# The last four gate quarters moved behind the first pair's scores, and one quarter ahead of every half batch of cached values

## The chip, the cores and the metric

The kernel runs on one core of one Trainium2 chip. The metric is the device time of one execution in microseconds; of before there are three timed runs, and one more execution that the hardware profiler recorded. The engines are named as in the profile: PE (TensorE matmuls), PEld (its weight loads), DVE (VectorE), ACT (ScalarE), POOL (GpSimd) and SP (SyncE, which only issues DMAs here).

## The reference, cut to what matters

One decoder layer for 512 prompt tokens and 8 x 4 sample tokens with the same weights. What the change touches is the part between the input projection and the output merge:

```
z = x @ w_in + b_in                     # q, k, v, conv pair ua/ub, gate_logits (2 x 1024 columns)
q, k = partial_rotary(q), partial_rotary(k)
u = ua * sigmoid(ub); conv = silu(layer_norm(causal_depthwise(u)))
prompt: s = q.k of 3 dilated groups, masked softmax, p @ v, groups merged by softmax denominators
sample: the same over cached keys and values, 8 batches, plus the 4 new tokens
y = (sigmoid(gA) * (attn @ w_attn_out) + sigmoid(gB) * (conv @ w_conv_out)) @ w_o
h = layer_norm(alpha*x + y);  out = layer_norm(alpha*h + moe(h))     # 32 experts, top 2
```

`gate_logits` are not needed before the merge. Their projection is the filler work that this change places differently.

## The kernel before, in words

Every engine has an instruction stream of its own, executed in the order in which it is written, and waits on semaphores. The program has these stages, by the profile's time: the input projection of 26 column tiles (to 171 us), the middle stage in which the gates are projected, q and k are rotated, and both attentions are computed (171 to 412 us), the merge with two projections, the first layer norm and the routing (to some 538 us), the loop over 32 experts, and the last layer norm.

**The middle stage.** The gate projection is cut into 64 quarters (`gate_quarter(q)`, L603): one unit `u = q // 2` is one 128-column tile of the gates over half of the tokens (272 of 544), eight matmuls deep, and a quarter is four of these (the profile shows each of them as two records, so a quarter is `x8`). Unit `u` accumulates in PSUM bank `u % 2`, signals `gate_mm` when its second quarter ends, and ACT copies it out with the bias (`gate_unit`, L1082), which signals `gate_free`. The first quarter of a unit waits until the unit two before it has been copied out.

A list, `order`, written out by hand in L369 to L384, sets what stands between the quarters. Each entry is (step, index, number of quarters ahead of it). PE, ACT and DVE walk the same list, each doing its own part of a step. The steps are:

- `conv_rows`: transposes of the last rows of the convolution's input (L613, L615).
- `rotate` 0 to 11 (L626): one matmul pair with the rotation matrix for each tile of q and k. DVE adds the parts (L1356 to L1359). The step's wait (`rot_used`) keeps PE at most two tiles ahead of DVE, whose first operation of each tile frees the bank pair. DVE comes to `rotate` only when it has finished the depthwise convolution (L1343), a loop that began under the projection.
- `values` 0 to 5 (L637): transposes of v; the first waits until DVE has rotated all 12 tiles (`rotated`).
- `sample_rows`, `cached_keys` 0 to 15 (L675), `keys`, `new_keys`, `sample_turn`, `sample_probs`: the sample attention up to its probabilities.
- `cached_values` 0 to 15 (L738): six matmuls of 8 or 2 columns each for each half batch, in banks 6 and 7; for the first two also three matmuls of 64 columns (L730).
- `conv_mean`, `conv_square`, `conv_var`, `conv_root`, `conv_silu`: the layer norm over channels, between half batches 3 and 13.
- `attend` 0 to 9: the prompt attention of 16 (row block, head) items in pairs. `scores(2p)` (L760, L762) writes banks 0 to 3 for two items; DVE masks and takes the maximum (L1437, L1439), ACT exponentiates (L1151), DVE normalises (L1445, L1446); `turn(i)` (L772) transposes the probabilities into banks 4 and 5, ACT copies them to SBUF (L1144), and `weigh(i)` (L786) multiplies them with the values. `turn(i)` for i of 1 and more waits for ACT's copy of the item before (`pt_act`), since both use banks 4 and 5.

In the list of before, `attend` 0 stands ahead of the last two half batches, and all 64 quarters stand ahead of `attend` 0. The convolution and the rotations get 7 + 12 quarters, `values` 7, the first three half batches of cached values 2 each, the others up to half batch 13 one each, and the last two none.

**Around it.** SP loads the weights of 8 quarters at a time, 8 quarters ahead. It loads `w_conv_out`, `w_o` and the first expert's weights when all 32 units are through (`gate_mm` of 32), because these overwrite the projection's operands. POOL issues the loads of cached keys and values four batches ahead.

Of the kernel before, what the change touches and what calls it, by code (L numbers as in the profile page):

```python
# [21 lines left out]
ACT = mybir.ActivationFunctionType  # L22
AX_X = mybir.AxisListType.X

P = 128
D = 1024
KD = D // P
SEQ, NB, NT = 512, 8, 4
NS = NB * NT
N = SEQ + NS  # L30
HALF = N // 2
# [78 lines left out]
def build(nc, a, o):  # L110
# [14 lines left out]
    with ExitStack() as ctx:  # L125
# [3 lines left out]
        def sem(name):  # L129
            return ctx.enter_context(nc.semaphore(name))  # L130
# [18 lines left out]
        ps = ctx.enter_context(nc.psum_tensor("ps", [P, 8, 512], F32))  # L149
# [11 lines left out]
        wring = eb[:, 0:4096].rearrange("p (s k n) -> p s k n", s=2, k=KD)  # L161
# [17 lines left out]
        zr = z2[:, :].rearrange("p (m n) -> p m n", n=N)  # L179
# [137 lines left out]
        gate_mm, gate_free, gate_sig = sem("gate_mm"), sem("gate_free"), sem("gate_sig")  # L317
# [48 lines left out]
        U_TILES = [2 * pair + c for pair in U_PAIRS for c in range(2)]  # L366


        order = [("conv_rows", 0, 7)] + [("rotate", m, 1) for m in range(12)] + [("values", m, 2 if m == 0 else 1) for m in range(6)]  # L369
        order.append(("sample_rows", 0, 1))  # L370
        for i in range(2 * NB):
            order.append(("cached_keys", i, 1))
# [2 lines left out]
        order += [("new_keys", 0, 0), ("sample_turn", 0, 1), ("sample_probs", 0, 3)]  # L375
        norm = {3: "conv_mean", 5: "conv_square", 7: "conv_var", 9: "conv_root", 12: "conv_silu"}
        for i in range(2 * NB):
            if i == 2 * NB - 2:
                order.append(("attend", 0, 0))
            order.append(("cached_values", i, (2 if i < 3 else 1) if i < 2 * NB - 2 else 0))  # L380
            if i in norm:
                order.append((norm[i], 0, 0))

        order += [("attend", p, 0) for p in range(1, 10)]  # L384
        assert sum(step[2] for step in order) == 4 * 16
        starts = np.cumsum([0] + [step[2] for step in order]).tolist()
        steps = [(kind, i, range(q, q + n)) for (kind, i, n), q in zip(order, starts)]

        STORES = 3 + 1 + NT + 3 * NT


# [151 lines left out]
        def _(pe):  # L543
# [27 lines left out]
            for h in range(2):  # L571
                pe.wait_ge(x_loaded[h], 32)
                for n in range(2):
                    for half in range(2):
                        for k in range(4 * h, 4 * h + 4):
                            last = pe.matmul(ps[:, 2 * n + half, 0:HALF], wring[:, 0, k, n * P:(n + 1) * P], xt[:, k, half * HALF:(half + 1) * HALF],
                                             start=k == 0, stop=k == KD - 1, skip_group_check=True)
# [13 lines left out]
            def gate_quarter(q):  # L591

                u = q // 2
                t, half, j = u // 2, u % 2, 13 + u // 4
                if q % 8 == 0:
                    pe.wait_ge(win_loaded[j % 2], 16 * (j // 2 + j % 2))
                if u < 2 and q % 2 == 0:

                    pe.wait_ge(tile_free, 2 + 25)
                elif q % 2 == 0:  # L600
                    pe.wait_ge(gate_free, u - 1)
                for k in range(4 * (q % 2), 4 * (q % 2) + 4):
                    last = pe.matmul(ps[:, half, 0:HALF], wring[:, j % 2, k, (t % 2) * P:(t % 2 + 1) * P],  # L603
                                     xt[:, k, half * HALF:(half + 1) * HALF], start=k == 0, stop=k == KD - 1, skip_group_check=True)
                if q % 2 == 1:
                    last.then_inc(gate_mm, 1)
# [138 lines left out]
            def scores(i):  # L745

                r, h = divmod(i, HEADS)
                hp = h // 2
                if i == 0:

                    pe.wait_ge(cnorm, 1)
                    pe.wait_ge(gate_free, 32)
                else:
                    pe.wait_ge(pmax, i)
                for g in range(3):
                    for odd in range(2):
                        rows, bank = slice(64 * odd, 64 * odd + 64), 2 - 2 * odd
                        q = zqkv[rows, Q0 + 2 * g + hp, r * P:(r + 1) * P]
                        if g == 0:
                            pe.matmul(ps[:, bank, :], q, zqkv[rows, K0 + hp, 0:SEQ], start=True, stop=True)  # L760
                            continue
                        last = pe.matmul(ps[:, bank + 1, (g - 1) * P:g * P], q, zqkv[rows, K0 + 2 * g + hp, r * P:(r + 1) * P],  # L762
                                         start=True, stop=True)
                        if g == 2:
                            last.then_inc(qk_ps, 1)

            def turn(i):
                pe.wait_ge(pnorm, i + 1)
                if i >= 1:
                    pe.wait_ge(pt_act, i)  # L770
                for c in range(6):
                    last = pe.transpose(ps[:, 4 + c // 3, (c % 3) * P:(c % 3 + 1) * P], prob[:, i % 4, c * P:(c + 1) * P], eye)  # L772
                last.then_inc(pt_ps, 1)
# [40 lines left out]
            for m in range(KD):  # L814
# [3 lines left out]
                for half in range(2):  # L818
# [3 lines left out]
                    for k in range(2):  # L822
                        last = pe.matmul(ps[:, s + 2 + half, 0:HALF], wa[:, k, m * P:(m + 1) * P], at[:, k, cols], start=k == 0, stop=k == 1)
# [84 lines left out]
            for t in range(NTT - 1):  # L908
                last = counts(t)
# [122 lines left out]
        def _(ac):  # L1032
# [29 lines left out]
            for n in range(8):  # L1062
                if n % 2 == 0 and n >= 2:

                    j = n // 2 + 1
# [12 lines left out]
            def gate_unit(u):  # L1078

                t, half = divmod(u, 2)  # L1080
                ac.wait_ge(gate_mm, u + 1)
                ac.activation(zr[:, 8 + t, half * HALF:(half + 1) * HALF], ps[:, half, 0:HALF], ACT.Identity,  # L1082
                              bias=colb[:, G0 + t:G0 + t + 1]).then_inc(gate_free, 1)

            def conv_rows(_):
# [857 lines left out]
```

## Time and profile before

| | us |
|---|---|
| timed runs, median of 3 (lowest to highest) | 1170.38 (1165.73 to 1170.91) |
| the profiled execution | 1171.49 |
| its span, first to last instruction | 1169.2 |
| PE busy in the span | 1107.1 (95%) |
| DVE busy | 841.0 (72%) |
| ACT busy | 581.9 (50%) |
| mean granted TensorE clock | 0.966 of full speed |

[...] A "busy" PE is one with an instruction under way; in the chain of waits each piece of time is given to the instruction or the releaser that the next step had to wait for, so the chain's durations of consecutive PE instructions add up without overlap, while those of a timeline overlap a little.

### The profile page before, as it was taken

To read this page: it belongs to the slowest core of one execution; us is meant where nothing else is said; L and a number is where in the kernel's file an instruction comes from. 1 tells how busy PE (TensorE), PEld (TensorE's weight loads), DVE (VectorE), ACT (ScalarE), POOL (GpSimd) and SP (SyncE) were. 2 spreads that over 40 slices of the span, in tenths; PEclk is the share of its full clock that TensorE was granted. 3 is DMA by queue.
4 is the path that set the end of the run, shared out by engine and by line. 5 is a ranking of instruction groups with operands and counts; after the bars stand their busy time and mean duration, and the time that the engine had idled before them with its cause. 6 is when DMAs were issued, how large, how long until landed. Compare 5 with 4: busy or idle time off the path is not lost.

```text
span 1169.2 us, 16215 instructions
## 1 busy us (share of the span) xinstructions
PE 1107.1 (95%) x6020; PEld 886.8 (76%) x6020; DVE 841.0 (72%) x988; ACT 581.9 (50%) x523; POOL 263.1 (22%) x185
## 2 busy tenths in 40 slices
PE   8999999999999999994999999999999999999970
PEld 7999998889888888863677777777777777777750
DVE  1699999500025728575799998888898888888857
ACT  2322211111115661003677778778777787787740
POOL 2453520000000015001032331332322323323200
PEclk8999999999998999995999999999999999999995
DMA  7468723235424440327799999999999999999824
GB/s 262 151 261 316 273 106 120 99 131 177 136 82 157 167 150 1 113 84 308 266 358 375 366 378 357 355 359 361 352 364 367 359 358 357 362 358 367 315 43 152
DMA packets 40481, 293.06 MB, mean 251 GB/s; under 512 B 10944, under 2 KB 14656, under 8 KB 24830
## 3 DMA queue, kind: packets, MB, share of 16 engines
q1 hardware_dynamic: 26173, 262.53, 59.4%
q0 software_dynamic: 10720, 25.98, 7.6%
q10 hardware_dynamic: 3552, 4.06, 1.1%
q8 instruction: 25, 0.41, 0.1%
q14 instruction: 11, 0.08, 0.0%
HBM read 286.83 MB, written 41.12 MB: 280 GB/s over the span
## 4 chain that ended last, share of the span: by engine, by line
PE 92%; DVE 4%; DMA 2%; issue 1%; ACT 0%; POOLq 0%; SPq 0%; DVEq 0%
PE ps L603 10%; PE ps L950 10%; PE ps L952 10%; PE ps L951 10%; PE ps L974 5%; PE ps L976 5%; PE ps L975 5%; PE ps L558 4%; PE ps L556 4%; PE ps L557 4%; PE ps L821 3%; PE ps L933 2%; PE ps L786 2%; PE ps L675 2%; PE ps L867 2%; PE ps L869 2%
## 5 line engine op out<-in xcount | busy, mean ns | idle before, releaser
L1675 DVE TENSOR_TENSOR region_b_split<-region_b,z_split 128x2048 fp32r<-128x2048 f32 x96 | 216.9, 2287 | 25.7 <-ACT z_split L1203 25.6
L1675 DVE TENSOR_TENSOR region_a_split<-region_a,z_split 128x2048 fp32r<-128x2048 f32 x96 | 216.7, 2286 | 23.2 <-ACT z_split L1203 23.1
L950 PE MATMUL ps<-z_split,scratch_split 128*96 128x512 f32 x512 | 206.2, 403 | 1.9 <-DVE scratch_split L1680 1.9
L952 PE MATMUL ps<-z_split,scratch_split 128*96 128x512 f32 x512 | 201.6, 394 | 0.0
L1203 ACT CAST z_split<-region_a 128x2048 fp32r<-128x2048 f32 x96 | 179.9, 1909 | 0.0
L1203 ACT CAST z_split<-region_b 128x2048 fp32r<-128x2048 f32 x94 | 176.2, 1908 | 2.0 <-PE ps L952 2.0
L1343 DVE SCALAR_TENSOR_TENSOR z_conv_gates<-scratch,column_vectors,z_conv_gates 128x512 f32<-128x512 f32 x240 | 142.8, 674 | 0.0
L603 PE MATMUL ps<-x_columns,region_b 128*128 128x272 f32 x512 | 129.4, 400 | 0.0
L558 PE MATMUL ps<-z_split,region_b_split 128*128 128x272 f32 x384 | 111.2, 290 | 0.0
L556 PE MATMUL ps<-z_split,region_b_split 128*128 128x272 f32 x384 | 110.8, 288 | 0.0
L952 PEld LDWEIGHTS ps<-z_split,scratch_split 128*96 128x96 f32 x512 | 83.0, 162 | 36.4
L950 PEld LDWEIGHTS ps<-z_split,scratch_split 128*96 128x96 f32 x512 | 85.1, 166 | 33.7 <-DVE scratch_split L1680 2.2
L557 PE MATMUL ps<-z_split,region_b_split 128*128 128x272 f32 x384 | 110.4, 287 | 0.0
L603 PEld LDWEIGHTS ps<-x_columns,region_b 128*128 128x128 f32 x512 | 95.5, 193 | 17.8
L974 PE MATMUL ps<-z_split,x_columns_split 128*96 128x512 f32 x256 | 101.0, 395 | 2.0 <-issue 1.2
L951 PE MATMUL ps<-region_b_split,scratch_split 128*96 128x512 f32 x256 | 101.0, 395 | 0.0
L976 PE MATMUL ps<-z_split,x_columns_split 128*96 128x512 f32 x256 | 100.9, 394 | 0.0
L951 PE MATMUL ps<-region_a_split,scratch_split 128*96 128x512 f32 x256 | 100.6, 393 | 0.0
L1778 POOL TENSOR_TENSOR region_b_split<-region_b,region_b_split 128x1024 fp32r<-128x1024 f32 x24 | 64.4, 2705 | 75.8 <-ACT region_b_split L1057 75.7
L1082 ACT ACTIVATE z_conv_gates<-ps,column_vectors 128x272 f32<-128x272 f32 x32 | 15.6, 488 | 123.3 <-PE ps L603 123.1
L1839 POOL DMA_INDIRECT expert_rows<-value_rows,block_rows x26 | 67.6, 2598 | 23.2 <-POOL block_rows L1836 23.2
L557 PEld LDWEIGHTS ps<-z_split,region_b_split 128*128 128x128 f32 x384 | 72.4, 189 | 0.0
(260 smaller groups left out, 1778.7 us busy)
## 6 DMA issues: line engine op xcount, KB each, us to landing
region_b<-in_w_expert_gate SPq DMA_DIRECT2D x16, 2048.0 KB, 12.7
region_a<-in_w_expert_up SPq DMA_DIRECT2D x16, 2048.0 KB, 13.0
region_a<-in_w_expert_gate SPq DMA_DIRECT2D x16, 2048.0 KB, 12.7
region_a<-in_w_expert_down SPq DMA_DIRECT2D x16, 2048.0 KB, 12.6
region_b<-in_w_expert_up SPq DMA_DIRECT2D x16, 2048.0 KB, 13.5
region_b<-in_w_expert_down SPq DMA_DIRECT2D x16, 2048.0 KB, 12.5
region_b<-in_w_in_pairs SPq DMA_DIRECT2D x20, 1024.0 KB, 4.8
region_b<-in_cache_tiles POOLq DMA_DIRECT2D x16, 768.0 KB, 4.9
```

The source lines that it names most:

```text
L556: pe.matmul(out, w_hi[:, s, k, tile], x_hi[:, k, cols], start=k == 0, stop=False)
L557: pe.matmul(out, w_hi[:, s, k, tile], x_lo[:, k, cols], start=False, stop=False)
L558: last = pe.matmul(out, w_lo[:, s, k, tile], x_hi[:, k, cols], start=False, stop=k == KD - 1)
L603: last = pe.matmul(ps[:, half, 0:HALF], wring[:, j % 2, k, (t % 2) * P:(t % 2 + 1) * P], xt[:, k, half * HALF:(half + 1) * HALF], start=k ...
L950: pe.matmul(out, xh[:, k, :], hi[:, k, :], start=k == 0, stop=False)
L951: pe.matmul(out, xh[:, k, :], lo[:, k, :], start=False, stop=False)
L952: last = pe.matmul(out, xl[:, k, :], hi[:, k, :], start=False, stop=k == KD - 1)
L974: pe.matmul(out, hh[:, k, :], hi[:, k, cols], start=k == 0, stop=False)
L976: last = pe.matmul(out, hl[:, k, :], hi[:, k, cols], start=False, stop=k == KF - 1)
L1203: ac.copy(high_part[w][:, part], raw[place][:, part]).then_inc(high_set[w], 1)
L1343: ve.scalar_tensor_tensor(dst, win(k), wdw_c[:, bass.ds(k * CT + c, 1)], dst, ALU.mult, ALU.add).then_inc(conv_step, 1)
L1675: ve.tensor_tensor(low_part[place][:, part], raw[place][:, part], high_part[high or w][:, part].bitcast(F32), ALU.subtract).then_inc(low_s ...
```

## The change

The quarters are spread over the list in another way, and the last four get other PSUM banks.

- `conv_rows` has 5 quarters ahead of it, no longer 7; `values` 0 has 1, no longer 2; the first three half batches of cached values have 1 each, no longer 2.
- The last two half batches have 1 quarter each, no longer none, and stand ahead of `attend` 0.
- `attend` 1 has the last 4 quarters (units 30 and 31) ahead of it; they stand behind `attend` 0's scores. These two units accumulate in banks 4 and 5, the banks of the turns, and wait for no bank. `scores(0)` therefore waits for 30 units copied out instead of 32, and `turn(0)` for all 32.

```diff
-        order = [("conv_rows", 0, 7)] + [("rotate", m, 1) for m in range(12)] + [("values", m, 2 if m == 0 else 1) for m in range(6)]
+        order = [("conv_rows", 0, 5)] + [("rotate", m, 1) for m in range(12)] + [("values", m, 1) for m in range(6)]
...
         for i in range(2 * NB):
-            if i == 2 * NB - 2:
-                order.append(("attend", 0, 0))
-            order.append(("cached_values", i, (2 if i < 3 else 1) if i < 2 * NB - 2 else 0))
+            order.append(("cached_values", i, 1))
...
-        order += [("attend", p, 0) for p in range(1, 10)]
+        order += [("attend", p, 4 if p == 1 else 0) for p in range(10)]
...
+        GATE_BANK = [u % 2 for u in range(30)] + [4, 5]
...
                 u = q // 2
+                bank = GATE_BANK[u]
...
-                elif q % 2 == 0:
+                elif q % 2 == 0 and u < 30:
                     pe.wait_ge(gate_free, u - 1)
...
-                    last = pe.matmul(ps[:, half, 0:HALF], wring[:, j % 2, k, (t % 2) * P:(t % 2 + 1) * P],
+                    last = pe.matmul(ps[:, bank, 0:HALF], wring[:, j % 2, k, (t % 2) * P:(t % 2 + 1) * P],
...
                     pe.wait_ge(cnorm, 1)
-                    pe.wait_ge(gate_free, 32)
+                    pe.wait_ge(gate_free, 30)
...
                 pe.wait_ge(pnorm, i + 1)
-                if i >= 1:
+                if i == 0:
+                    pe.wait_ge(gate_free, 32)
+                else:
                     pe.wait_ge(pt_act, i)
...
-                ac.activation(zr[:, 8 + t, half * HALF:(half + 1) * HALF], ps[:, half, 0:HALF], ACT.Identity,
+                ac.activation(zr[:, 8 + t, half * HALF:(half + 1) * HALF], ps[:, GATE_BANK[u], 0:HALF], ACT.Identity,
```

**PE around the first rotations.** L603 is a gate quarter (4 matmuls here), L613 and L615 are `conv_rows`, L626 is `rotate`. Before:

```order
L603 MATMUL ps<-x_columns,region_b 128x272 [waits gate_free]
L603 MATMUL ps<-x_columns,region_b 128x272 x7
L603 MATMUL ps<-x_columns,region_b 128x272 [waits gate_free]
L603 MATMUL ps<-x_columns,region_b 128x272 x3
L613 MATMUL ps<-const_small,scratch 30x128 [waits state_sb,u_set]
```

```order
L626 MATMUL ps<-region_a,const_small 128x272 x2
L603 MATMUL ps<-x_columns,region_b 128x272 x4
L626 MATMUL ps<-region_a,const_small 128x272 [waits rot_used]
L626 MATMUL ps<-region_a,const_small 128x272
L603 MATMUL ps<-x_columns,region_b 128x272 [waits gate_free]
```

And now, the same place in the program:

```order
L603 MATMUL ps<-x_columns,region_b 128x272 [waits gate_free]
L603 MATMUL ps<-x_columns,region_b 128x272 x3
L613 MATMUL ps<-const_small,scratch 30x128 [waits state_sb,u_set]
L613 MATMUL ps<-const_small,scratch 30x128 x3
L615 MATMUL ps<-const_small,region_a 32x128 x4
L603 MATMUL ps<-x_columns,region_b 128x272 x4
L626 MATMUL ps<-region_a,const_small 128x272 [waits tile_free]
L626 MATMUL ps<-region_a,const_small 128x272
L603 MATMUL ps<-x_columns,region_b 128x272 [waits gate_free]
L603 MATMUL ps<-x_columns,region_b 128x272 x3
L626 MATMUL ps<-region_a,const_small 128x272 x2
```

Behind the run of quarters, `conv_rows` now follows after two quarters fewer. From there on the two orders are alike to the last rotation: one quarter between two of them, and `rot_used` waited for from `rotate` 2 on.

**PE from the last rotation to the first values (L637).** Before:

```order
L626 MATMUL ps<-region_a,const_small 128x272 [waits rot_used]
L626 MATMUL ps<-region_a,const_small 128x272
L603 MATMUL ps<-x_columns,region_b 128x272 x4
L603 MATMUL ps<-x_columns,region_b 128x272 [waits gate_free]
L603 MATMUL ps<-x_columns,region_b 128x272 x3
L637 MATMUL ps<-const_small,region_a 128x128 [waits rotated]
```

Now:

```order
L626 MATMUL ps<-region_a,const_small 128x272 [waits rot_used]
L626 MATMUL ps<-region_a,const_small 128x272
L603 MATMUL ps<-x_columns,region_b 128x272 x4
L637 MATMUL ps<-const_small,region_a 128x128 [waits rotated]
L637 MATMUL ps<-const_small,region_a 128x128 x3
```

One quarter instead of two stands between the last rotation and the step that waits for DVE's last rotation.

**PE at the last half batches and the first pair.** L738 is `cached_values`, L760 and L762 are `scores`, L772 (now L774) is `turn`, L786 (now L788) is `weigh`. Before:

```order
L760 MATMUL ps<-region_a 128x512 [waits gate_free,cnorm]
L760 MATMUL ps<-region_a 128x512
L762 MATMUL ps<-region_a 128x128 x4
L738 MATMUL ps<-w_attn,region_b 128x8 [waits cache_loaded3]
L738 MATMUL ps<-w_attn,region_b 128x2 x4
L738 MATMUL ps<-w_attn,region_b 128x8 x2
L738 MATMUL ps<-w_attn,region_b 128x2 x4
L738 MATMUL ps<-w_attn,region_b 128x8
L760 MATMUL ps<-region_a 128x512 [waits pmax]
L760 MATMUL ps<-region_a 128x512
L762 MATMUL ps<-region_a 128x128 x4
L772 MATMUL ps<-const_small,scratch 128x128 [waits pnorm]
```

Now:

```order
L603 MATMUL ps<-x_columns,region_b 128x272 x4
L738 MATMUL ps<-w_attn,region_b 128x8
L738 MATMUL ps<-w_attn,region_b 128x2 x4
L738 MATMUL ps<-w_attn,region_b 128x8
L760 MATMUL ps<-region_a 128x512 [waits gate_free,cnorm]
L760 MATMUL ps<-region_a 128x512
L762 MATMUL ps<-region_a 128x128 x4
L603 MATMUL ps<-x_columns,region_b 128x272 x16
L760 MATMUL ps<-region_a 128x512 [waits pmax]
L760 MATMUL ps<-region_a 128x512
L762 MATMUL ps<-region_a 128x128 x4
L774 MATMUL ps<-const_small,scratch 128x128 [waits gate_free,pnorm]
```

The 12 short matmuls between the first two pairs' scores are gone from there, and 16 gate matmuls stand in their place.

## Rows read from the trace of the kernel before

**Rows 1.** Page, part 4: the chain that ended last, by engine

```profile
PE 92%; DVE 4%; DMA 2%; issue 1%; ACT 0%; POOLq 0%; SPq 0%; DVEq 0%
```

**Rows 2.** Windows of PE: start:end us, length, busy (x), clock, DMA share, GB/s

```profile
238.70:289.80 51.10, 51.10 (x337) 1.00 0.54 173
311.40:314.84 3.44, 3.44 (x9) 0.50 0.45 135
316.90:360.40 43.50, 43.50 (x267) 1.00 0.17 56
366.05:372.85 6.80, 5.82 (x30) 0.50 0.65 238
374.00:412.00 38.00, 38.00 (x334) 1.00 0.48 195
410.00:430.00 20.00, 18.89 (x93) 1.00 0.67 218
```

**Rows 3.** Chain of waits, conv_rows to first values: start us, us, what

```profile
185.23 1.83 PE ps L603 x8
...
192.57 0.92 PE ps L626 x4
...
218.24 3.67 PE ps L603 x16
221.90 0.44 PE ps L637 x4
```

**Rows 4.** Timeline of DVE: start us, us, engine, line, operation [idle before]

```profile
169.78 20.05 DVE L1343 SCALAR_TENSOR_TENSOR z_conv_gates<-scratch,column_vectors,z_conv_gates 128x32 f32<-128x32 f32 x49
190.05 0.72 DVE L1356 TENSOR_TENSOR value_rows<-ps,region_b 128x544 f32<-128x544 f32 x1 [0.22 <-DVE z_conv_gates L1343]
...
218.27 0.72 DVE L1356 TENSOR_TENSOR value_rows<-ps,region_b 128x544 f32<-128x544 f32 x1 [0.63 <-PE ps L626]
...
219.66 0.73 DVE L1359 TENSOR_TENSOR region_a<-region_a,value_rows 128x544 f32<-128x544 f32 x1
...
300.09 0.54 DVE L1391 COPY w_attn<-ps 32x384 f32<-32x384 f32 x1
```

**Rows 5.** Chain of waits, first half batches of cached values

```profile
299.58 3.67 PE ps L603 x16
...
309.26 0.81 PE ps L730 x6
310.07 1.44 PE ps L738 x12
311.50 5.46 PE ps L603 x16
```

**Rows 6.** Timeline of PE, the last two half batches

```profile
361.87 2.85 PE L738 MATMUL ps<-w_attn,region_b 128*128 128x8 f32 x24
```

**Rows 7.** Chain of waits, first pairs of the prompt attention

```profile
366.52 1.49 PE ps L772 x6
...
368.02 0.81 ACT z_conv_gates L1144
...
368.97 1.51 PE ps L772 x6
370.48 2.53 PE ps L786 x12
```

**Rows 8.** Chain of waits, the second pair and the end of the attention

```profile
374.51 0.81 PE ps L772 x6
375.32 1.34 PE ps L786 x12
...
412.21 1.11 issue
```

**Rows 9.** Timeline of ACT: the copy of the last gate unit

```profile
359.23 0.49 ACT L1082 ACTIVATE z_conv_gates<-ps,column_vectors 128x272 f32<-128x272 f32 x1 [1.16 <-PE ps L603]
```

**Rows 10.** Timeline of SP: the load of w_conv_out

```profile
367.57 0.38 SPq L462 DMA_DIRECT2D x_columns<-in_w_conv_out  x1
```

## The prediction

> **What bounds the kernel now.** I read the chain of waits by engine first: PE holds 92% of it [rows 1]. In the middle stage, which the change reorders, the chain is PE instruction after PE instruction, so the total work on PE is fixed and only three things can change the time: where PE waits, where it runs at the lower clock, and what later stages get from it. Then I read windows of PE for the granted clock and for idle time [rows 2]. [...] Last I read the chain and DVE's timeline at the places where `order` changes [rows 3 to 8], because a filler that is taken away uncovers what it hid.
>
> **What the quarters removed early had hidden.** Two quarters go from ahead of `conv_rows`. It ended at 185.23; a quarter takes 1.83 us there [rows 3], so everything behind it comes 3.66 us earlier. `rotate` 0 and 1 wait for no result of DVE's rotations, so they simply move. `rotate` 2 stood at 192.57 and would stand at 188.91. But it waits until DVE has read the banks of `rotate` 0, and DVE is in the convolution until 189.8, starts its first rotation at 190.05 and finishes that operation at 190.77 [rows 4]. DVE's convolution began under the projection, which the change leaves alone, so this time does not move. PE waits 190.77 - 188.91 = 1.9 us, and since it takes its matmuls in order, the quarters behind cannot fill the wait. After it PE again needs 2.75 us for one tile (1.83 + 0.92), and DVE some 2.15 as in the last one [rows 3, 4], so DVE catches up and nothing more is lost: +1.9.
>
> One quarter goes from ahead of `values` 0, which waits for DVE's last rotation. That began as PE's last rotation ended (218.27) and ended at 219.66 + 0.73 = 220.39, 2.15 us behind PE's [rows 3, 4]. Two quarters (3.67) covered it; one covers 1.83. PE waits 2.15 - 1.83 = 0.3 us more: +0.3.
>
> The three quarters taken from half batches 0 to 2 hid nothing that is late. Half batch 0 waits for DVE's copies of the probabilities: the quarters ahead of it began at 299.58 and the second copy ended at 300.09 + 0.54 = 300.63 [rows 4, 5], 1.05 us later, under the one quarter that is left: 0. Between the steps of the convolution's norm stand as many quarters as before, and two more half batches with their quarters stand between it and `scores(0)`, so that wait gets looser: 0.
>
> **What the last quarters do.** The two last half batches move from between the first two pairs' scores to ahead of them, each with a quarter. Their 2.85 us [rows 6] lay beside DVE's maxima, for which `scores(2)` waits; 4 quarters of 1.83 us, 7.3 together, lie there now and cover that and the exponentials and the normalising as well. PE did not wait at `scores(2)` in the trace, so this cover gives nothing: 0. ACT's two copies of units 30 and 31 take 0.49 each [rows 9]; the last one lies under `scores(2)`, which ran from 361.87 + 2.85 = 364.72 to 366.52, 1.8 us [rows 6, 7], ahead of `turn(0)`, which needs it: 0. On ACT they stand behind the first pair's exponentials and ahead of the copy of `turn(0)`, and all of that is over by then. Banks 4 and 5 have been free since the sample's probabilities were copied. `scores(0)` now waits for 30 units; the last of these ends one half batch ahead of it: 0.
>
> The wait between `turn(0)` and `turn(1)` stays. `turn(1)` waits until ACT has copied `turn(0)`'s result (PE's idle time from 368.01 to 368.97, with ACT's copy of 0.81 in it [rows 7]); nothing is put between these two. Whoever expects the quarters to fill that hole will not find it filled.
>
> SP's load of `w_conv_out` was issued at 367.57 [rows 10]. With 2.2 us of new waits the quarters end at about 366.5, so it starts within a microsecond or so of where it did, and it is needed behind the attention, past 412: 0. Everything behind 412 moves as a block.
>
> **The clock.** In the trace it fell at 366.05, after PE had run the two half batches back to back (2.85 us of matmuls of 8 and 2 columns) and a short pair of scores, and it stayed low over both turns, the wait between them and `weigh(0)`. There `turn(0)` took 1.49, `turn(1)` 1.51, `weigh(0)` 2.53 [rows 7]; at full clock a turn takes 0.81 and a `weigh` 1.34 [rows 8]. That is 0.68 + 0.70 + 1.19 = 2.6 us. In the changed kernel 7.3 us of full matmuls precede this place and no half batch stands next to another one without a quarter between. I take it that the fall goes: -2.6.
>
> The other fall, at 311.40, came behind three matmuls of 64 columns and the six short ones of half batch 1 (0.81 + 1.44), and two quarters took 5.46 instead of 3.67: 1.8 us [rows 3, 5]. It came behind half batch 1 and not behind half batch 0, which is the same work. The changed kernel has both of them, at other times, so I leave this at 0, between -1.8 (no fall) and +1.8 (a fall behind both).
>
> A fall may also come beside the new wait of 1.9 us. The trace has no such wait there. The lower bound is none: the wait of 1.11 us at 412.21 was followed by full clock [rows 2, 8]. The upper bound is one stretch like that of 311.40, 3.44 us at half the rate, 1.7 us. The wait is nearly twice the harmless one, so I take the middle: +0.9.
>
> [...]
>
> **The sum.** +1.9 + 0.3 - 2.6 + 0.9 = +0.5 us, on the profiled execution's 1171.49: 1172.0. That execution lies 1.1 us above the median of the timed runs, so against the median it is 1170.38 + 0.5 = 1170.9. What a measurement of this kernel can tell from no change is about 0.5%, 5.9 us: the sum is a tenth of it.
>
> **The rivals.**
> - *No new waits of weight, and the clock better than before.* The fall at 366 goes, that at 311.40 does not come again, and the wait at `rotate` 2 brings none: 2.2 - 2.6 - 1.8 = -2.2, so 1168.2. For it: the fall behind half batch 1 did not come behind half batch 0. Against it: both half batches are still there. 0.25.
> - *Slower: the wait for DVE at `rotate` 2 costs more than itself.* PE's clock falls beside it, and the stretch around the two turns falls again, because the 0.98 us wait and the transposes are still there. Then nothing is gained: 2.2 + 1.7 = +3.9, so 1174.3. It is slower than before from the point where the stretch at 366 is not saved, for then the 2.2 us of waits stand alone. Against it: the later pairs run the same turns at full clock for 38 us [rows 2]. 0.18.
> - *Slower by more than can be overlooked: single quarters no longer hold the clock.* If the clock fell behind every other of the 16 half batches, 8 stretches of 1.7 us would come: 2.2 - 2.6 + 13.6 = +13, so 1183.6; from four further stretches on it passes 0.5%. Against it: 16 half batches of cached keys with single quarters ran for 51.10 us, and later those of values for 43.50 us, at 1.00 [rows 2]. 0.03.
> - *The change doesn't do what it says: the quarters in banks 4 and 5 hold up the pair behind them.* If the last unit's copy were late for `turn(0)`, PE would wait 0.49 us plus what ACT has ahead of it, at most one exponential; that is under 1.5 us and lies in the forecast's own range. Against it: 1.8 us of scores stand between.
>
> **How the numbers follow.** Forecast 0.54, its own range 1169 to 1172.7; better clock 0.25; clock worse 0.18; much worse 0.03. The 80% range reaches to 1166.5, since the timed runs of before themselves go down to 1165.73, and to 1174.5, which takes in the second rival. Faster by over 0.5% needs 1164.5 or less, which no case gives by itself, though the runs of before spread by 5 us: 0.06. Slower by over 0.5% is 1176.2 or more: the third rival and a little of the second, 0.06. The rest, 0.88, is within 0.5%.
>
> **What would show it.** In the profile after: a PE idle time of about 1.9 us ahead of the third rotation, released by DVE's L1358 (L1356 before), and one of 0.3 ahead of the first values; `turn(0)` at 0.8 us and `weigh(0)` at 1.34; a wait of about 1 us on ACT between `turn(0)` and `turn(1)`, unchanged; no wait ahead of `scores(2)`; the 0.50 stretches counted anew. The prediction is wrong if PE does not wait at the third rotation, if the gate matmuls in banks 4 and 5 make `turn(0)` wait, or if the time from 412 on (the merge and the experts) changes its length by more than a microsecond or two.

## The result and the profile after

The changed kernel took 1175.99 us (median of 20 executions, 1168.64 to 1179.47), the kernel before beside it 1166.49 (20 executions, 1165.57 to 1172.23). The ratio is 1.0064 with a 95% interval of 1.0048 to 1.0081: it is slower by 0.64%, some 7.5 us. That is how far the means lie apart (1175.39 and 1167.80); the medians are 9.5 us apart. The forecast was 1170.9 us and no change that can be told.

Both medians need a look at the executions behind them. Of the 20 of before, 13 lie at 1165.6 to 1167.1 and 7 at 1170.4 to 1172.2. The trace of before that the prediction started from (1171.49) belongs to the 7. The changed kernel's spread over 11 us, and its recorded execution (1171.72, mean clock 0.969) is one of the quicker ones. The time goes roughly with the mean clock: 1168.6 at 0.972, 1171.7 at 0.969, 1176.2 and 1176.5 at 0.966 and 0.964, 1179.4 at 0.964.

In the recorded execution most of what the working said of the middle stage is found again; two terms of the clock are not. First PE's waits in that stage, by releaser (us in total, times, longest):

```profile
PE ps L626 <- DVE value_rows L1358: 2.1, 1, 2.1
PE ps L823 <- issue: 1.1, 1, 1.1
PE ps L774 <- ACT z_conv_gates L1146: 1.0, 1, 1.0
PE ps L637 <- DVE region_a L1361: 0.4, 1, 0.4
```

The first and the last are new: PE stands 2.1 us ahead of the third rotation and 0.4 us ahead of the first values, as the two steps on the uncovered waits had it (1.9 and 0.3). The wait between the first two turns is what it was [rows 7]: 1.0 us here, and 6.80 - 5.82 = 0.98 before [rows 2]. The chain of waits at the three places (start us, us, what):

```profile
191.13 1.18 PE ps L626 x4
192.31 3.52 PE ps L603 x8
195.84 0.92 PE ps L626 x4
...
220.18 0.74 DVE region_a L1361
220.92 0.04 issue
220.96 0.66 PE ps L637 x4
```

```profile
300.69 0.81 PE ps L730 x6
301.50 1.44 PE ps L738 x12
302.94 1.94 PE ps L603 x8
```

```profile
358.87 1.06 PE ps L760 x4
359.93 0.44 PE ps L762 x8
360.38 7.53 PE ps L603 x32
367.91 1.06 PE ps L760 x4
368.97 0.44 PE ps L762 x8
369.41 0.82 PE ps L774 x6
370.23 0.02 issue
370.25 0.81 ACT z_conv_gates L1146
371.06 0.14 issue
371.19 0.85 PE ps L774 x6
372.04 1.34 PE ps L788 x12
```

The reader is to see three things. Behind the wait, the quarter at 192.31 takes 3.52 us where 1.83 is usual: a fall of the clock beside the wait, by the full 1.7 us where the sum had 0.9. The half batches with their single quarters (L730 and L738 with one L603 between, from 300.69 us on) run at full clock in this execution, so the fall that the trace of before had at 311.40, and that the sum left in place, is missing. The turns and `weigh(0)` run at full clock too (0.82, 0.85, 1.34 against 1.49, 1.51, 2.53 in [rows 7]). The clock records of all 14 traces hold 1.00 and 0.50 of full speed and no other value; a fall is a stretch at 0.50. The windows of PE show the three places in the columns of [rows 2]:

```profile
192.24:195.64 3.40, 3.40 (x9) 0.50 0.27 111
196.00:222.00 26.00, 25.62 (x115) 1.00 0.11 41
300.70:358.90 58.20, 58.20 (x358) 1.00 0.29 99
374.00:412.00 38.00, 38.00 (x333) 1.00 0.44 177
```

PE's hole behind the attention comes at 412.59, 0.38 us later than in [rows 8]; the sum had said 0.5. That the two agree is in part luck. From the end of the first values (222.34 us before, 221.62 now, with three quarters, 5.5 us, fewer ahead of it) one reads a loss of 4.8 us: 1.7 of the clock, 0.2 because the first quarter began later (171.52 against 171.37), and the rest, 2.9 us, for the two waits, where the sum had 2.2. With -2.6 at the turns and -1.8 at half batch 1 that gives 2.9 + 1.7 + 0.2 - 2.6 - 1.8 = +0.4. Two terms were too small and one that helped was left out.

What lies behind the hole is the same length in both (758.2 and 758.0 us to the end of the execution, reckoned from the merge's first matmul). So this pair of traces is explained, but the distance between the medians is not in it: it pairs one of the slower executions of before with one of the quicker ones of the changed kernel.

### The profile page after: what moved, and what is told of

Its sections match the earlier page's. It is cut to its first block, busy times and chain, and to the rows that moved or that the text cites. A ratio compares the mean times of both kernels' runs of the same rounds, so it can differ in the third digit from the quotient of the medians.

```text
span 1169.4 us, 16216 instructions
## 1 busy us (share of the span) xinstructions
PE 1105.4 (95%) x6020; PEld 884.3 (76%) x6020; DVE 841.1 (72%) x988; ACT 581.6 (50%) x523; POOL 263.0 (22%) x185
## 4 chain that ended last, share of the span: by engine, by line
PE 79%; DVE 8%; issue 8%; DMA 2%; DVEq 1%; ACT 1%; POOLq 0%; SPq 0%
PE ps L952 10%; PE ps L954 10%; PE ps L953 10%; PE ps L603 9%; PE ps L976 5%; PE ps L978 5%; PE ps L977 5%; DVE z_conv_gates L1345 4%; PE ps L823 3%; PE ps L935 2%; PE ps L788 2%; PE ps L738 2%; PE ps L675 2%; PE ps L869 2%; PE ps L871 2%
## 5 line engine op out<-in xcount | busy, mean ns | idle before, releaser
L603 PE MATMUL ps<-x_columns,region_b 128*128 128x272 f32 x512 | 130.2, 401 | 0.0
L603 PEld LDWEIGHTS ps<-x_columns,region_b 128*128 128x128 f32 x512 | 95.1, 192 | 17.6
```

Of the source, the lines that this page charges most:

```text
L603: last = pe.matmul(ps[:, bank, 0:HALF], wring[:, j % 2, k, (t % 2) * P:(t % 2 + 1) * P], xt[:, k, half * HALF:(half + 1) * HALF], start=k ...
```

## The experiments

Two theories, stated ahead of the runs. **Theory A**: the wait for DVE at the third rotation, and the fall of the clock beside it, make the change slow. **Theory B**: with a single quarter ahead of each half batch of cached values the clock falls there in most executions. Each kernel was run several times beside the kernel before; kernels in one group shared a chip and the runs of before. Every execution lists its mean clock, and one of each is traced. The runs of before fall in the same two kinds everywhere: of 109 in all, those of the first comparison included, 57 lie below 1169 us and the others above. Where the clock is listed, the first have 0.969 to 0.974 and the others 0.965 to 0.969. The shares differ, and with them the median of before: 1167.12 us beside the next four kernels, 1169.93 beside the four from "The wait alone" to the first filled kernel, 1169.79 beside the last four. The ratios are therefore the fairer measure, and a forecast that stands on 1166.5 is to be read with care.

### The changed kernel again

No edit; for a trace of another execution.

> The changed kernel once more, for a second trace. Its executions spread from 1168.6 to 1179.5 us with a mean granted clock from 0.972 down to 0.964, and its recorded trace is a quick one. If the spread is the clock's, a trace of a slow execution shows more stretches at 0.50 at the same work. Theory A (waits): they lie at the third rotation and at the turns. Theory B (single quarters): they lie among the half batches of cached keys or values, which now have one quarter each. Median expected about 1176.

1176.69 us (8 runs, 1168.59 to 1178.51), ratio 1.0066 (1.0040 to 1.0091). The traced execution took 1176.38. Its chain at the half batches:

```profile
304.50 0.81 PE ps L730 x6
305.30 1.44 PE ps L738 x12
306.74 2.59 PE ps L603 x8
309.33 2.36 PE ps L738 x12
311.69 3.48 PE ps L603 x8
315.18 1.24 PE ps L738 x12
```

and two windows of its PE:

```profile
191.82:195.12 3.30, 3.30 (x9) 0.50 0.34 142
307.94:314.30 6.36, 6.36 (x22) 0.50 0.38 124
```

The fall beside the wait is there, and behind half batch 1 another one. It is 6.8 us long (the second window takes in most of it) and costs (2.59 - 1.94) + (2.36 - 1.24) + (3.48 - 1.94) = 3.3 us, where the one of before cost 1.8 [rows 5]. At the lower clock a half batch of short matmuls takes 2.36 us instead of 1.24, and with one quarter between two of them the clock was back at 1.00 only after the 6.8 us. Both theories have their place in this trace.

### 7 quarters at conv_rows

```diff
-        order = [("conv_rows", 0, 5)] + [("rotate", m, 1) for m in range(12)] + [("values", m, 1) for m in range(6)]
+        order = [("conv_rows", 0, 7)] + [("rotate", m, 1) for m in range(12)] + [("values", m, 1) for m in range(6)]
-        order += [("attend", p, 4 if p == 1 else 0) for p in range(10)]
+        order += [("attend", p, 2 if p == 1 else 0) for p in range(10)]
```

> 7 quarters ahead of conv_rows again, 2 instead of 4 behind the first scores; the rest as changed. Takes away the wait of 2.1 us ahead of the third rotation. Theory A (that wait and the fall of the clock beside it make the change slow): 1.9 to 2.1 us of the wait and 1.7 us of clock come back, and the slow executions with them: about 1168 to 1170. Theory B (single quarters ahead of the half batches let the clock fall): only the wait comes back, about 1174.

1170.06 us (12 runs, 1166.65 to 1174.96), ratio 1.0021 (1.0002 to 1.0039). The wait and the fall beside it are gone from the trace (the 0.4 us ahead of the first values stay), and two thirds of the loss with them: more than the 3.8 us of the two by themselves. So far A. But five of the twelve executions took 1171.9 or more, and the traced one (1172.99) has the longest low stretch seen so far in this stage (L692 is `conv_mean`):

```profile
305.84 2.85 PE ps L603 x8
308.69 2.36 PE ps L738 x12
311.05 3.83 PE ps L603 x8
314.88 2.36 PE ps L738 x12
317.24 5.38 PE ps L692 x16
```

```profile
306.72:320.36 13.64, 13.64 (x44) 0.50 0.67 234
```

That is B, without any wait for DVE in its neighbourhood: 0.9 + 1.1 + 1.9 + 1.1 + 1.6 = 6.6 us (`conv_mean` takes 3.77 at full clock).

### 7 and 2 quarters, single ones only at the half batches

```diff
-        order = [("conv_rows", 0, 5)] + [("rotate", m, 1) for m in range(12)] + [("values", m, 1) for m in range(6)]
+        order = [("conv_rows", 0, 7)] + [("rotate", m, 1) for m in range(12)] + [("values", m, 2 if m == 0 else 1) for m in range(6)]
-        order += [("attend", p, 4 if p == 1 else 0) for p in range(10)]
+        order += [("attend", p, 1 if p == 1 else 0) for p in range(10)]
```

> 7 quarters ahead of conv_rows and 2 ahead of the first values, as before; 1 quarter ahead of each half batch and 1 behind the first scores. No wait for DVE is left. Theory A: about 1166 to 1168, at or below the kernel before. Theory B: 1172 to 1174, a wide spread, clock down to 0.964 in some executions.

1173.31 us (6 runs, 1173.00 to 1175.55), ratio 1.0058 (1.0039 to 1.0078). A said 1166 to 1168 and is refuted as the only cause; B said 1172 to 1174. In the traced execution the low stretch begins at 304.1 us and lasts over 10 us. A part, 0.8 us, is a new wait: with one quarter behind the first scores, `scores(2)` waits for DVE's maxima.

### Two quarters ahead of half batches 0 and 1

```diff
-            order.append(("cached_values", i, 1))
+            order.append(("cached_values", i, 2 if i < 2 else 1))
-        order += [("attend", p, 4 if p == 1 else 0) for p in range(10)]
+        order += [("attend", p, 2 if p == 1 else 0) for p in range(10)]
```

> As changed, but 2 quarters ahead of half batches 0 and 1, and 2 instead of 4 behind the first scores. The waits for DVE stay (2.5 us). Theory A: as the changed kernel, about 1176. Theory B: the spread shrinks to that of before and the median lies near 1170.

1173.70 us (6 runs, 1173.17 to 1180.12), ratio 1.0075 (1.0047 to 1.0103). B's forecast of a median near 1170 missed, and so did A's 1176 by the median, though the ratio is that of the changed kernel again. Two quarters did not prevent a fall. What the trace shows is that it was over sooner with them, after 3.4 us where the three traces above had 6.8, 13.6 and over 10. It begins at 304.5, and the chain reads

```profile
302.09 0.81 PE ps L730 x6
302.90 1.44 PE ps L738 x12
304.34 5.46 PE ps L603 x16
309.79 0.81 PE ps L730 x6
```

as in [rows 5]: two quarters take 5.46 instead of 3.77 us, 1.7 us for the fall, and behind them the clock is up again. Two of the six executions took 1180.1, and none of those is traced, so what they have more is open.

### The wait alone, in the kernel before

```diff
-        order = [("conv_rows", 0, 7)] + [("rotate", m, 1) for m in range(12)] + [("values", m, 2 if m == 0 else 1) for m in range(6)]
+        order = [("conv_rows", 0, 5)] + [("rotate", m, 1) for m in range(12)] + [("values", m, 2 if m == 0 else 1) for m in range(6)]
-        order += [("attend", p, 0) for p in range(1, 10)]
+        order += [("attend", p, 2 if p == 1 else 0) for p in range(1, 10)]
```

(with the banks and waits of the changed kernel for the last units)

> The kernel before with one part of the change alone: 5 quarters instead of 7 ahead of conv_rows, the other 2 behind the first scores (banks 4 and 5). Half batches as before (2, 2, 2, then 1, and none between the first two pairs' scores). Theory A (the wait for DVE at the third rotation and the fall of the clock beside it cost): +2.1 for the wait and +1.7 for the fall on the 1166.5 to 1167 of before, about 1170.5. Theory B (single quarters ahead of the half batches): within 2.2 us of before, 1167 to 1169.

1170.82 us (12 runs, 1169.76 to 1174.70), ratio 1.0025 (1.0009 to 1.0040). The number 1170.5 is met, but it was added up on the quick executions of before. By the ratio the loss is 2.9 us (1.1 to 4.7), which has the expected 3.8 in it. The trace has the wait of 2.1 us and, in this stage, one stretch at 0.50, from 190.1 to 193.5 us. No execution came below 1169.8, where before reaches 1165.3: all of them lie over 4 us above its quickest.

### The single quarters alone, in the kernel before

```diff
-            order.append(("cached_values", i, (2 if i < 3 else 1) if i < 2 * NB - 2 else 0))
+            order.append(("cached_values", i, 1 if i < 14 else 0))
-        order += [("attend", p, 0) for p in range(1, 10)]
+        order += [("attend", p, 3 if p == 1 else 0) for p in range(1, 10)]
```

> The kernel before with another part alone: 1 quarter instead of 2 ahead of half batches 0, 1 and 2, the other 3 behind the first scores. No wait for DVE. Theory A: as before, 1166 to 1168. Theory B: the clock falls around half batches 0 and 1 and stays at 0.50 for 7 us and more, median 1170 to 1173 and stretches at 0.50 between 300 and 320 us in the trace.

1171.64 us (12 runs, 1167.31 to 1174.77), ratio 1.0019 (1.0002 to 1.0037). There is no new wait. The quickest execution is 2.1 us above the quickest of before and the median 1.7 above; A said none, B a median of 1170 to 1173. The lower end of the interval is close to no change. The traced execution is that quickest one. It has no fall between 300 and 320 us, where B wanted one, and one of 3.4 us at 356.5, behind the last two half batches, which stand back to back there as in the kernel before; what the slower eleven have is not shown here. So this run supports B by its time and not by its trace.

### No wait at the rotations and no thin half batches

```diff
-        order = [("conv_rows", 0, 5)] + [("rotate", m, 1) for m in range(12)] + [("values", m, 1) for m in range(6)]
+        order = [("conv_rows", 0, 7)] + [("rotate", m, 1) for m in range(12)] + [("values", m, n) for m, n in enumerate((2, 1, 1, 1, 0, 0))]
...
-        order += [("new_keys", 0, 0), ("sample_turn", 0, 1), ("sample_probs", 0, 3)]
+        order += [("new_keys", 0, 0), ("sample_turn", 0, 1), ("sample_probs", 0, 2)]
...
-            order.append(("cached_values", i, 1))
+            order.append(("cached_values", i, 2 if i < 3 else 1))
...
-        order += [("attend", p, 4 if p == 1 else 0) for p in range(10)]
+        order += [("attend", p, 1 if p == 1 else 0) for p in range(0, 10)]
```

> Half batches 14 and 15 ahead of the first scores with a quarter each, 1 quarter behind the scores, and neither wait nor thin half batches: 7 quarters at conv_rows, 2 at the first values, 2 ahead of half batches 0 to 2; the three quarters come from the last two values (none there) and from sample_probs (2 instead of 3), where DVE is early. Both theories: no new loss. If the fall of the clock at the first pair's turns, which a third of the runs of before seem to have, goes, then the median stays at 1166 to 1167 and the runs at 1170 to 1172 get rare.

1169.22 us (12 runs, 1167.91 to 1171.17), ratio 1.0003 (0.9989 to 1.0016): level with before, not at the 1166 to 1167 that was expected; its lowest execution is 2.7 us above the lowest of before. With one quarter behind the first scores it also has the wait of 0.8 us at `scores(2)`. The trace shows two falls, behind half batches 0 and 1, each ended by the two quarters behind it:

```profile
300.82:304.20 3.38, 3.38 (x10) 0.50 0.00 0
307.66:311.00 3.34, 3.34 (x9) 0.50 0.96 289
```

So with two quarters as well, the clock fell (at 300.8 and 307.7 us) within 1.1 us behind the run of three matmuls of 64 columns and six of 8 and 2. In each of the eight traces that have a fall between 299 and 312 us, the first one begins at the end of such a run or within 1.1 us behind it.

### The wait filled with extra matmuls, twice and with a control

```diff
+                if m == 2:
+                    pe.wait_ge(u_sb, 1)
+                    for k in range(4):
+                        pe.matmul(ps[:, 7, 0:HALF], rot, zqkv[:, 2, 0:HALF], start=True, stop=True, skip_group_check=True)
                 if m >= 2:
                     pe.wait_ge(rot_used, m - 1)
```

> The changed kernel with 4 extra matmuls of 272 columns (their result is not used) ahead of the third rotation, 1.8 us of work in the wait of 2.1 us. If the fall of the clock at 192 us comes from PE's idle time there, it goes, and 1.7 us with it: 1176 becomes 1174 or so, and the trace has 1.00 from 184 to 222 us. If the fall has another cause, it stays and nothing moves.

1169.67 us (12 runs, 1168.40 to 1175.99), ratio 1.0013 (0.9998 to 1.0029). The fall beside the wait is gone: the windows of PE are

```profile
184.00:222.00 38.00, 37.39 (x167) 1.00 0.20 68
296.00:364.00 68.00, 68.00 (x408) 1.00 0.30 100
```

With 2.1 us of idle time there the fall came, with 0.2 us it did not, and nothing else there changed: here it hung on PE's idle time. But the median is some 4 us below the 1174 that was expected: 11 of 12 executions lie at 1168.4 to 1170.2, which hardly leaves room for a fall at the single quarters either, and neither theory had that. The changed kernel had run on another chip, so the filled one was run again beside it:

> The changed kernel a third time, as the control for the filled kernels, which so far ran on another chip than it. If the filled kernel's good time (1169.7 median, mean clock 0.974 in most executions) was the chip's, this comes near 1171 to 1172 here (the filled kernel without its 1.8 us of extra matmuls plus the fall beside the wait). If it was the filler's, this stays at 1175 to 1177.

> The filled kernel once more, on the same chip as the control: 4 extra matmuls of 272 columns ahead of the third rotation. If the filler removes the falls behind it as well as that beside the wait: 1169 to 1170 again, 5 to 6 us below the control. If it removes only the one fall of 1.7 us: the control less 1.7.

The control is the changed kernel. It took 1172.64 us (12 runs, 1168.57 to 1179.19; 1.0039, 1.0015 to 1.0062). Its traced execution (1173.43) has the wait of 1.9 us, the fall beside it at 190.8 and another of 6.8 us from 306.8 on. The filled kernel took 1169.65 (12 runs, 1168.63 to 1179.43; 1.0024, 1.0003 to 1.0046). Now three of its twelve executions took 1176.6 or more, and the traced one of these (1176.64) has falls at 300 (3.4 us long, with a single quarter behind it) and from 306.7 to 320.3 us. The filler does not shut out the later falls. Whether it makes them rarer is not settled. Side by side, 3 of its 12 executions and 6 of the control's 12 are above 1173 us, which can be chance; the means differ by 1.6 us (1171.61 and 1173.23), about what the one fall beside the wait costs, the smaller of the two effects expected. Over all groups it is 4 of 24 against 27 of 40, but on different chips, and beside the filled kernel the changed one was itself 3.4 us quicker by the median than in the first comparison.

### The filled kernel, 1.8 us later

The same 4 matmuls once more, ahead of the first values.

> The filled kernel with a second set of 4 extra matmuls ahead of the first values (1.8 us more work, put behind the last wait for DVE). It brings the half batches 1.8 us later, about where the fall beside the wait put them in the changed kernel, with no fall at 192 us. If the later falls depend on when the half batches come: falls between 300 and 320 us return, 1174 or more. If they do not: the filled kernel's time plus 1.8, about 1171.5, clock mostly 0.974.

1175.56 us (12 runs, 1171.58 to 1180.33), ratio 1.0059 (1.0040 to 1.0078). By the ratios that is 4.1 us above the filled kernel (by the medians 5.9) for 1.8 us of work, and the mean clock is at 0.971 or less in all of them, where eight of the filled kernel's twelve have 0.972 or more. So the clock falls more often, or for longer, in the kernel whose half batches come 1.8 us later. It fits two others: the kernel with 7 and 2 quarters has its half batches 1.8 us later than that with 7 and 1, and took 3.3 us more, of which 0.8 is its wait at `scores(2)`. But where the added falls lie is not shown, as the traced execution (1171.58) is the quickest and has no fall in this stage; and the executions of one kernel differ by nearly as much as the shift (half batch 0 begins at 300.69 us in one trace of the changed kernel and at 299.40 in the control's). What decides in which execution the clock falls stays open.

### Short runs split

Half batches 0 and 1 have one quarter ahead, and one between the 64-column matmuls and the short ones; 1 quarter everywhere else; 7 at `conv_rows`; values 2, 1, 1, 1, 0, 0; `sample_probs` 2; 2 behind the first scores.

```diff
                                   skip_group_check=True)
+                    gate_quarter(between)
                 if hp == 0:
                     pe.wait_ge(cache_loaded[b % 4], 16 * (b // 4 + 3))
```

> A version that should beat both: no wait for DVE (7 quarters at conv_rows, 2 ahead of the first values), in half batches 0 and 1 one quarter ahead and one between the three matmuls of 64 columns and the six short ones, 1 ahead of every other half batch, 2 behind the first scores; the missing quarters come from the last two values and from sample_probs. If runs of short matmuls make the clock fall, there are none of 2.2 us left: 1165 to 1166.5 in nearly every execution, where before has 1165.5 in half of them and 1170 to 1172 in the rest.

1166.67 us (12 runs, 1165.38 to 1167.85), ratio 0.9988 (0.9973 to 1.0002). It is the quickest of the variants, and no execution is above 1167.9, while 18 of the 35 of before beside it are at 1169 or more (means 1166.65 and 1168.74). By the interval it is not yet proven faster than before; it is clearly faster than the changed kernel beside it, whose interval is 1.0015 to 1.0062. The chain at the half batches, and one window over the whole middle stage:

```profile
294.78 0.81 PE ps L730 x6
295.59 2.03 PE ps L603 x8
297.62 1.24 PE ps L739 x12
298.85 1.94 PE ps L603 x8
300.79 0.81 PE ps L730 x6
301.60 2.03 PE ps L603 x8
```

```profile
184.00:412.00 228.00, 225.91 (x1420) 1.00 0.38 131
```

No fall, and the only idle time is the two old holes. The single quarters at the other 14 half batches did no harm once the two long runs were split. Against the kernel of "No wait at the rotations" it changes the split, one quarter fewer at half batch 2 and one more behind the first scores; that last one takes away 0.8 us, and by the ratios the two lie 1.8 us apart.

## Why the prediction was wrong

The time of 1175.99 us lies above the 80% range, 1166.5 to 1174.5, and the change is slower beyond its interval, where no change was forecast. A loss of over 0.5% had a chance of 0.06.

**What the quarters removed early had hidden: right.** 1.9 and 0.3 us were worked out, 2.1 and 0.4 of idle time measured. In the chain the two cost 2.9 us together, 0.7 more than the 2.2 of the sum: besides the idle time, the rotation and the values behind it took 1.18 and 0.66 us instead of 0.92 and 0.44.

**The fall beside the new wait: half its size.** The prediction took the middle, +0.9, between nothing and 1.7. All three traces of the changed kernel, that with two quarters at half batches 0 and 1 and that of the wait alone show it in full, 1.7 us, and the filler took it away. The middle of two outcomes that are each all or nothing was not the likelier value; the row that it was compared with, the 1.11 us behind the attention [rows 8], was too short a wait to say anything about one of 2. One thing is open: 7 of the 40 executions of the changed kernel took only 1168.6 to 1169.1 us, at 0.972. That is 3.0 to 3.7 us above the quickest of before beside them, less than the 4.6 of waits and fall together. None of them is traced, so whether the fall is missing there is not shown.

**The quarters behind the first scores, and the fall at 366 us: right in the traces, wrong as a gain.** The turns ran at full clock and nothing waited, as said. But -2.6 us was credited against a trace of 1171.49, and 13 of the 20 executions of before, at 1165.6 to 1167.1, can hardly have that loss. (No quick one of before is traced; the split kernel's trace has the same time and clock, 1165.49 at 0.972, and no fall in this stage.) The spread of the three timed runs (1165.73, 1170.38, 1170.91) and the two falls in the trace, 1.8 + 2.6 = 4.4 us, stood ahead of the prediction, and the runs' distance of 5 us is near that. The step "that execution lies 1.1 us above the median" should have read: the traced execution is one of two kinds of execution, and the gain exists in one kind only.

**The single quarters: the step that failed.** The prediction left the fall at 311.40 at 0, between -1.8 and +1.8, on the ground that both kernels have the two half batches. That the single quarters no longer hold the clock was a rival with a chance of 0.03, priced at +13, against which stood 51.10 and 43.50 us of single quarters at full clock [rows 2]. Those rows have only short runs of 1.24 us, or 1.69 with the step `keys`; they say nothing about the two of 0.81 + 1.44, where the second quarter was taken away. There a fall mostly lasts 7 to 14 us and costs 3.3 to 6.6, not 1.8. The term put at 0 measured -1.8 in the trace of 1171.72, where no fall came, and 3.3 for the fall in the traces of 1176.38 and 1173.43. The rival was the right kind of loss at the wrong place and with too small a chance.

The sum from what was measured in the trace of 1176.38: 2.9 of waits, 1.7 beside them, 3.3 for the fall behind half batch 1, on the 1166.5 of before: 1174.4. The other 2.0 us lie for the most part behind the attention. Against the trace of 1171.72 the stage ends 3.0 us later (415.54 against 412.59), and 1.7 more lie behind it. There the stretch at 0.50 around the merge and the routing is 34 us long instead of 31. First the trace of 1176.38, then that of 1171.72:

```profile
529.80:563.80 34.00, 17.76 (x96) 0.50 0.70 270
526.80:557.40 30.60, 14.89 (x89) 0.50 0.77 301
```

The change leaves that part of the program alone, and the wait alone in the kernel before has the same longer stretch in its trace, so the 1.7 us are not shown to be the change's.

**The clock and the kind of work.** The clock fell beside 2 us of idle time and behind runs of short matmuls (0.81 + 1.44 us), and there a half batch took 2.36 us that takes 1.24 at full clock. The split kernel adds that four full matmuls (one quarter, 2.03 us there) between two short runs of 0.81 and 1.24 us were enough in its traced execution, which stands at 1.00 from 184 to 412 us.

## What to carry to other kernels

The filler work on TensorE had two jobs here. It covered waits (taken away, it left 2.1 us idle at the third rotation), and the clock stayed up with it: 3.4 us at 0.50 came beside that wait, and none in the three traces in which the wait was filled. A list that moves such work is to be read for both: ask at each place from which it is taken what other engine's result comes next, and how long a run of short matmuls is left. When timed runs fall in two groups, find out to which one the trace belongs before pricing a gain from it. Here a run of small matmuls (0.81 + 1.44 us) was better cut in two by one batch of large ones than followed by two batches: ratio 0.9988 against 1.0003, some 1.8 us, of which 0.8 belongs to the quarter behind the first scores.

## What the runs showed of the hardware

- A wait of PE of 1.9 to 2.1 us was followed by one stretch of 3.4 us at half the clock in all five traces that have it (three of the changed kernel, two of experiments); with the same place filled by 1.8 us of matmuls and 0.2 us or less left idle it was not, in three traces. No wait of 1.0 to 1.2 us at the turns or behind the attention was followed by one.
- The length of a wait did not decide alone. At the start of the projection PE waits 3.2 to 3.9 us for its first operands in all 14 traces. A stretch at 0.50 comes with it in 11 of them and not in three (waits of 3.38 us in the kernel with 7 and 2 quarters, 3.19 in that with two quarters at half batches 0 to 2, 3.28 in the first filled one), while the split kernel has one at 3.16.
- The clock fell without a gap in PE's work too: in 8 of the 13 traces that have the run of 0.81 + 1.44 us of short matmuls undivided, a fall begins at its end or within 1.1 us behind it. Behind the runs of 1.24 us with a quarter on either side none begins in the 14 traces.
- At half batches 0 and 1 a stretch at half the clock lasted 3.4 us where two quarters followed (four stretches in three traces), and 6.8 to 13.6 us where single quarters alternated with short matmuls (five stretches; a sixth, in the second filled kernel, ended after 3.4).
- 1.8 us of further work ahead of the half batches cost 4.1 us by the ratios (1.0024 and 1.0059), with a lower mean clock. Why is open.
